# Gated linear attention on one Trainium2 core: masked level scores summed by GpSimd and a reduction instead of merged by predicated copies

## The reference

```python
def step(s, blk):
    qc, kc, vc, gc = blk
    G = jnp.cumsum(gc, axis=2)
    decay = jnp.exp(jnp.where(tri, G[:, :, :, None, :] - G[:, :, None, :, :], -jnp.inf))
    scores = jnp.einsum('bhik,bhjk,bhijk->bhij', qc, kc, decay)
    o = jnp.einsum('bhij,bhjv->bhiv', scores, vc) + jnp.einsum('bhik,bhkv->bhiv', qc * jnp.exp(G), s)
    G_last = G[:, :, -1:, :]
    s = s * jnp.exp(G_last)[:, :, 0, :, None] + jnp.einsum('bhjk,bhjv->bhkv', kc * jnp.exp(G_last - G), vc)
    return s, o
```

## Time and profile before

| | us |
|---|---|
| median of the runs | 3316.45 |
| lowest run | 3316.24 |
| the profiled execution | 3316.24 |
| its span | 3314.4 |

### The profile page before, as it was taken

One profiled execution on the slowest core, in us unless ns is written; L12 is line 12 of the kernel. 1 busy time (PEld: TensorE's weight loads), 2 busy tenths in 40 slices (PEclk: granted clock), 3 DMA queues, 4 the chain that ended last, 5 costly groups with the idle time before them and its releaser, 6 DMA issues.

```text
span 3314.4 us, 41712 instructions
## 1 busy us (share of the span) xinstructions
PE 3104.0 (94%) x18192; PEld 1768.4 (53%) x18192; DVE 785.8 (24%) x1628; ACT 415.2 (13%) x1028; POOL 280.8 (8%) x344
## 2 busy tenths in 40 slices
PE   6989899999989999899989999978999999999998
PEld 2456644444457777576656766454444434444443
DVE  1136821000037667400142000253000000000002
ACT  1014220000022221200030000130000000000001
POOL 1121300000003323300000000000000000000030
PEclk9999989999999999899989999978999999999998
DMA  8670012122121222235323443305899999999992
GB/s 345 249 277 2 1 64 76 38 95 82 50 62 45 64 64 71 101 118 194 122 96 114 159 178 114 117 26 231 341 405 359 358 388 380 358 361 407 357 378 104
DMA packets 210613, 609.15 MB, mean 184 GB/s; under 512 B 6076, under 2 KB 53404, under 8 KB 203904
## 3 DMA queue, kind: packets, MB, share of 16 engines
q1 hardware_dynamic: 204912, 592.20, 47.0%
q0 software_dynamic: 5056, 13.67, 1.2%
q10 hardware_dynamic: 464, 0.60, 0.1%
HBM read 600.28 MB, written 6.16 MB: 183 GB/s over the span
## 4 chain that ended last, share of the span: by engine, by line
PE 81%; DVE 8%; issue 3%; ACT 3%; DMA 2%; another core or an unknown queue 1%; POOL 1%; PEld 0%; POOLq 0%; ACTq 0%; PEldq 0%; DVEq 0%
PE ps_ffn_gate L610 10%; PE ps_ffn_up L610 10%; PE ps_ffn_down L646 10%; PE ps_moe_down L3011 6%; PE ps_moe_gate L2966 6%; PE ps_moe_up L2966 6%; PE ps_odd L1920 4%; PE ps_lin L1400 4%; PE ps_moe_down L3017 3%; PE ps_moe_up L2971 3%; PE ps_moe_gate L2971 3%; PE ps_lin L296 3%; PE ps_project L528 3%; PE ps_ple_gate L2593 2%; DVE rec_qd L2179 2%
## 5 line engine op out<-in xcount | busy, mean ns | idle before, releaser
L610 PE MATMUL ps_ffn_gate<-hT,ring_buf 128*128 128x256 f32 (+1 forms) x1152 | 343.5, 452 | 4.3 <-issue 2.3
L610 PE MATMUL ps_ffn_up<-hT,ring_buf 128*128 128x256 f32 (+1 forms) x1152 | 336.8, 445 | 1.5 <-DMA ring_buf<-in_w_ffn_up_dram 0.2
L646 PE MATMUL ps_ffn_down<-ring_buf,ffn_hiddenT 128*128 128x512 f32 x752 | 325.9, 593 | 3.0 <-issue 3.0
L610 PEld LDWEIGHTS ps_ffn_gate<-hT,ring_buf 128*128 128x128 f32 x1152 | 221.9, 194 | 120.3 <-issue 98.9
L610 PEld LDWEIGHTS ps_ffn_up<-hT,ring_buf 128*128 128x128 f32 x1152 | 217.8, 190 | 110.8 <-issue 90.0
L1920 PE MATMUL ps_odd<-ring_buf,hT 128*128 128x256 f32 (+2 forms) x1024 | 236.1, 385 | 8.0 <-ACT hg_kT L2055 6.4
L646 PEld LDWEIGHTS ps_ffn_down<-ring_buf,ffn_hiddenT 128*128 128x128 f32 x752 | 141.7, 190 | 182.0 <-issue 182.0
L695 DVE TENSOR_TENSOR ffn_hiddenT<-ffn_silu_buf,ps_ffn_up 128x256 f32<-128x256 f32 (+1 forms) x72 | 36.2, 503 | 728.1 <-PE ps_ffn_up L610 728.1
L3143 DVE TENSOR_TENSOR moe_hidden_buf<-moe_silu_buf,ps_moe_up 128x768 f32<-128x768 f32 (+1 forms) x32 | 27.3, 854 | 747.7 <-PE ps_moe_up L2971 727.2
L1920 PEld LDWEIGHTS ps_odd<-ring_buf,hT 128*128 128x128 f32 x1024 | 173.7, 192 | 55.1 <-ACT hg_kT L2055 7.9
L2966 PE MATMUL ps_moe_up<-ring_buf,moe_xg_buf 128*64 128x512 f32 (+1 forms) x1024 | 199.5, 542 | 0.1
(11 more groups left out here) (511 smaller groups left out, 3363.5 us busy)
## 6 DMA issues: line engine op xcount, KB each, us to landing
ring_buf<-in_w_exp_up_dram SPq DMA_DIRECT2D x24, 4096.0 KB, 16.6
ring_buf<-in_w_exp_down_dram SPq DMA_DIRECT2D x24, 4096.0 KB, 16.3
moe_third<-in_w_exp_gate_dram SPq DMA_DIRECT2D x16, 4096.0 KB, 17.8
mod_pieces<-in_mod_w_dram SPq DMA_DIRECT2D x40, 1024.0 KB, 6.5
ring_buf<-in_w_exp_gate_dram SPq DMA_DIRECT2D x8, 4096.0 KB, 17.5
ring_buf<-in_odd_w_in_dram SPq DMA_DIRECT2D x40, 512.0 KB, 5.3
moe_third<-in_w_exp_gate_dram SPq DMA_DIRECT2D x8, 2048.0 KB, 10.9
ring_buf<-in_w_exp_up_dram SPq DMA_DIRECT2D x8, 2048.0 KB, 7.8
```

The costliest lines, as they stand in the source:

```text
L610: mm = nc.tensor.matmul(ps[:, 0:wide], view[:, k, i * P:(i + 1) * P], hT[:, k, first_col:first_col + wide], start=k == 0, stop=k == KD - 1)
L646: mm = nc.tensor.matmul(ps_y[i % 2][:, h, :], hidT[:, b, i * P:(i + 1) * P], view[:, b, h * 512:(h + 1) * 512], start=first, stop=end)
```

## The change

`merge` is replaced by three steps.

- DVE, `mask`: two instructions, one for each head, multiply all 8 levels with their masks out of PSUM into `masked` in SBUF, 1024 elements each. Each raises `rec_masked`, which now counts two a unit. `masked` has one buffer, so mask(u) waits for `rec_summed` of the unit before.
- GpSimd, `halves`: two instructions, each behind its mask, add levels 4 to 7 onto 0 to 3, 512 elements each, and raise `rec_halved`.
- DVE, `add_levels`: one reduction over the four remaining levels, 1024 elements to 256, into `summed` (two buffers), which raises `rec_summed`.

TensorE's output then has one product for each head in place of two. In DVE's queue add_levels(u) stands behind queries(u+2) and take(u-1); in GpSimd's queue halves(u) stands ahead of keys(u+2), and the first two calls of `root` stand between halves(14) and halves(15). Of the gates of the first pair of heads four go ahead of the last reduction.

```diff
-        PLACES, ROUNDS = 2, NL // 2
+            summed = flat[:, 3072:3584].rearrange("p (b e n) -> p b e n", b=2, e=2)
-            merged = tail(1, 0, 2 * 2 * PLACES * P).rearrange("p (b e s n) -> p b e s n", b=2, e=2, s=PLACES)
+            masked = tail(1, 0, 2 * NL * P).rearrange("p (e l n) -> p e l n", e=2, l=NL)
...
-                    pe.wait_ge(S["rec_masked"].handle, S["rec_masked"].at(u))
+                    pe.wait_ge(S["rec_masked"].handle, S["rec_masked"].at(2 * u))
...
-                    pe.wait_ge(S["rec_masked"].handle, S["rec_masked"].at(u + 1))
+                    pe.wait_ge(S["rec_summed"].handle, S["rec_summed"].at(u + 1))
                     pe.wait_ge(S["rec_state"].handle, S["rec_state"].at(u))
                     if not fresh(u):
                         nc.tensor.matmul(ps_out, qd[:, u % 3, 0, :], state[:, d, :, :], start=True, stop=False)
                     for e in range(2):
-                        for s in range(PLACES):
-                            mm = nc.tensor.matmul(ps_out[:, e, :], merged[:, u % 2, e, s, :], vs(u, e),
-                                                  start=fresh(u) and s == 0,
-                                                  stop=s == PLACES - 1 and (fresh(u) or e == 1))
+                        mm = nc.tensor.matmul(ps_out[:, e, :], summed[:, u % 2, e, :], vs(u, e), start=fresh(u),
+                                              stop=fresh(u) or e == 1)
...
+                def halves(u):
+                    for e in range(2):
+                        pool.wait_ge(S["rec_masked"].handle, S["rec_masked"].at(2 * u + e + 1))
+                        nc.gpsimd.tensor_tensor(masked[:, e, 0:4, :], masked[:, e, 0:4, :], masked[:, e, 4:8, :],
+                                                ALU.add).then_inc(S["rec_halved"].handle, 1)
...
-                for u in range(2, n):
-                    keys(u)
-                root(1, 0, 4, slice(0, 2))
-                root(2, 0, 2, slice(2, 4))
+                for u in range(n):
+                    halves(u)
+                    if u + 2 < n:
+                        keys(u + 2)
+                    if u == n - 2:
+                        root(1, 0, 4, slice(0, 2))
+                        root(2, 0, 2, slice(2, 4))
...
-                def merge(u):
-
-                    d, mine = units[u][1], merged[:, u % 2, :, :, :]
+                def mask(u):
                     dve.wait_ge(S["rec_scores"].handle, S["rec_scores"].at(u + 1))
+                    dve.wait_ge(S["rec_summed"].handle, S["rec_summed"].at(u))
+                    for e in range(2):
+                        nc.vector.tensor_tensor(masked[:, e, :, :], ps_scores[:, e, :, :], T.mask[:, units[u][1], :, :],
+                                                ALU.mult).then_inc(S["rec_masked"].handle, 1)
+
+                def add_levels(u):
+                    dve.wait_ge(S["rec_halved"].handle, S["rec_halved"].at(2 * u + 2))
                     if u >= 2:
                         dve.wait_ge(S["rec_out"].handle, S["rec_out"].at(u - 1))
-                    for r in range(ROUNDS):
-                        levels = slice(r * PLACES, (r + 1) * PLACES)
-                        made_by = ps_scores[:, :, levels, :]
-                        which = T.mask[:, d, levels, :].unsqueeze(1).to_broadcast([P, 2, PLACES, P])
-                        if r == 0:
-                            last = nc.vector.tensor_tensor(mine, made_by, which, ALU.mult)
-                        else:
-                            last = nc.vector.copy_predicated(mine, which.bitcast(I32), made_by)
-                        if r < ROUNDS - 1:
-                            link_v(last)
-                    last.then_inc(S["rec_masked"].handle, 1)
+                    nc.vector.tensor_reduce(summed[:, u % 2, :, :], masked[:, :, 0:4, :].rearrange("p e l n -> p e n l"),
+                                            AX.X, ALU.add).then_inc(S["rec_summed"].handle, 1)
...
                 for u in range(n):
-                    merge(u)
+                    mask(u)
                     if u + 2 < n:
                         queries(u + 2)
                     if u >= 1:
                         take(u - 1)
-                gated(0, range(4), 1)
+                    if u == n - 1:
+                        gated(0, (0, 1), 1)
+                    add_levels(u)
+                gated(0, (2, 3), 1)
                 gated(1, (0, 1), 2)
                 take(n - 1)
```

More of the change, by code:

```diff
@@ L989, in _ @@
                 link_v(gated(1, (2,), 4))
-            for k in ("rec_sums", "rec_decays", "rec_q", "rec_k", "rec_scores", "rec_masked", "rec_out",
+            for k in ("rec_sums", "rec_decays", "rec_q", "rec_k", "rec_scores", "rec_summed", "rec_out",
                       "rec_state"):
                 S[k].passed(n)
+            for k in ("rec_masked", "rec_halved"):
+                S[k].passed(2 * n)
             for k in ("rec_qk_psum", "rec_qk_ready"):
```

## The result

| | before | changed |
|---|---|---|
| median of the runs, us | 3316.34 | 3350.51 |
| lowest run, us | 3312.14 | 3347.82 |
| the span read here, us | 3314.4 | 3350.1 |

What follows compares the result with a forecast made beforehand. TensorE was taken to set the pace of the pairs stage, a third of a microsecond a round over DVE. Rounds +30.6, round without queries +0.7 and tail +2.6 give +34 on 3316.24: 3350 us, range 3331 to 3366.

Steps and rivals of the forecast that it cites:

- TensorE's saving: In the pairs stage, TensorE's output product loses 0.445 us a unit, hidden unless DVE also gets under 5.8 us.
- The port: In steady rounds, GpSimd's additions and DVE's queries exclude each other at SBUF, costing 1.27 us a round.
- the 14 rounds: Pairs stage, from the first mask to that of unit 14: 110.1 us against 79.45, so +30.6.
- free queries: Rival, chance 0.10: additions and queries don't wait for each other; round 6.77 us, 18 us less, 3332.
- reduction blocked: Rival, chance 0.06: DVE's reduction waits for GpSimd's keys from 6.04 to 7.14 us; 15 us more, 3365.
- Keys first: Rival, chance 0.08: GpSimd runs keys(u+2) right after the second addition, ahead of the waiting query; 29 us more, 3379.
- they alternate: At the SBUF port, GpSimd and DVE take turns one after the other; the reason given against "Keys first".
- The round: DVE's steady round in the pairs stage, from first mask to next first mask: 8.04 us.
- The reduction's price: DVE's reduction of 1024 elements to 256 costs 1.90 us, from the odd layer's row with the same access pattern.
- The clock: Granted clock stays 1.00 in the stage; rival, chance 0.04: it falls to 1.2 GHz, 38 us more, 3388.
- the end after the take stays: Behind the last take of the pairs stage nothing changes: 0 us.

Runs made afterwards that it cites:

- the doubled product: Changed kernel with TensorE's product of the summed scores issued twice for each head: 3349.35 us, ratio 1.0116.
- The two orders of DVE's queue: Changed kernel with DVE's queue reordered: take(u-1) before queries(u+2), 3364.97 us; or queries at the end of the round, after the reduction, 3340.76 us.
- the levels innermost: Changed kernel with the levels innermost in the masked buffer, so masks write with a stride and the reduction reads neighbours: 3351.62 us, ratio 1.0122.
- take ahead of the queries: Changed kernel with take(u-1) placed before queries(u+2) in DVE's queue, nothing else: 3364.97 us, ratio 1.0162.
- two other executions: Changed kernel with TensorE's product of summed scores issued twice (3349.35 us), and with 36 and 30 idle TensorE products around the last output (3347.64 us).
- the merge in the odd layer: Kernel before with the odd layer's mask, addition and reduction replaced by the merge of the pairs: 3313.12 us, ratio 1.0004.

## Why the prediction was right

- **TensorE's saving is worth nothing.** Right: the doubled product left the first 13 rounds alone to 0.01 us. Even alone in the kernel before it brought nothing in the end, which I had not seen.
- **The port.** Right in place, order and size: L932 at 2.29 us in the steady rounds, its end 1.09 after the additions, keys held to 3.07. The two orders of DVE's queue moved the 14 rounds by +14.2 and -7.6 us where the same turns gave +15 and -11. The collision costs 1.17 us a round; 1.27 was worked out. The rivals "free queries" and "reduction blocked" fall with these three kernels. "Keys first" does not happen in the changed kernel, but the reason given against it, "they alternate", does not hold everywhere: with the levels innermost DVE has two turns running. The order of coming fits all rows: L932 had come before the keys here, and where it came later (take ahead of the queries, and the late 14th rounds) the keys did go first.
- **The round.** 8.04 worked out, 7.95 measured. The second addition ended 3.84 us into the round, not 3.99: it ends 1.13 behind L931 where one alone takes 1.27, as L932 ends 1.09 behind an addition where it takes 1.22 alone, so some 0.13 of a waiting instruction seems to pass during the wait (an estimate from these rows). The rest holds: take 1.06, reduction 1.92 on average (1.90), next mask 0.10 on.
- **The reduction's price.** Right at 1.9, and right for the reason given, the same access pattern. The Trainium skill ("VectorE: DVE Perf Modes", the perf-mode tier table) has this instruction in the slowest mode, one element a cycle, an estimated 1.07 us for 1024. The trace's 1.22 with the levels innermost is near that; the 1.92 of the strided read is not, and there the measurement decides.
- **The clock.** Wrong in what it would show. I forecast 1.00; the stage has 0.92 and 0.73, with stretches at the lower level of 1.2 GHz. Inside the rounds of the changed kernel's execution this was free, since TensorE had slack: in the timeline above the scores take 3.35 us (granted clock 0.51) instead of 1.83, and the next mask still comes 7.95 us on. In two other executions it was not: the 14th round took 9.95 and 9.93. Behind the stage the clock cost 2.2 us, which the step "the end after the take stays" had at nothing.
- **Luck.** The 14 rounds were over-estimated by 1.9 us: 14 x 0.09 = 1.3 by the second addition and the gaps, and 0.5 by four rounds of 7.82 us, whose take copies a fresh state. The 2.2 us behind the stage, unforeseen, made up for them. So the agreement of 3350 with 3350.51 is closer than the working deserves, by about 2 us: without the stretch behind the stage the places add up to 32.1 us, and with it to 34.3.

The 28.7 us of the 14 rounds split by rows: L931 and L932 are 0.10 and 1.07 us longer, 14 x 1.17 = 16.4. Masks and reduction take 2.27 + 2.04 from start to start where the merge had 3.01, 14 x 1.30 = 18.2. That is 34.6, and DVE's busy time did rise by 34.5 (71.74 to 106.23). The 28.7 are less because DVE's idle time fell from 79.45 - 71.74 = 7.7 us to 108.19 - 106.23 = 2.0: it no longer waits for TensorE.

## What to carry to other kernels

Before work is moved to GpSimd, look at what DVE does at that very time: an instruction with two SBUF operands beside a busy GpSimd costs the whole remainder of that neighbour, and an order of the queue in which one-operand or PSUM work meets GpSimd gives part of it back. Work out who comes to the port first: here a delay of a third of a microsecond cost 2 us. Cost the replacement against the engine that is full: here TensorE was full by a third of a microsecond and DVE next, so a saving on the one bought at 1.3 us on the other could only lose. A strided operand made the reduction 1.6 times and the mask 1.7 times as long, and turning the layout only moved the stride to the writer. And look at the place as well as at the total: the merge in the odd layer is 6.5 us in a trace, and nothing in the median.

## What the runs showed that was not expected

- Taking 0.445 us a round from the engine that set the pace of most rounds did not shorten the kernel: in the profiled execution the granted clock went to 0.75 in the last rounds, and these lost 3.1 us where the first twelve had gained 2.85.
- Idle products in the stage's tail, 5.1 us of them ahead of the last output and 4.2 behind it, made the work that follows 10.5 instead of 13.8 us long.
- A float32 mask of 1024 elements out of PSUM costs 1.22 us with contiguous writes and 2.02 with writes 32 bytes apart; a GpSimd addition of 512 elements costs 1.27 either way, contiguous or in runs of four.
- DVE and GpSimd do not strictly alternate at the port: in 14 of 14 rounds with the levels innermost DVE ran both query products, and the addition that had started together with the second waited for it.
- The odd layer is 6.5 us shorter in the trace with the merge of the pairs, and the median of the runs does not show it.
